# Value products of two heads made together in an attention stage on one core

## The reference

```python
p = softmax(q @ k.T * scale)          # branches B (windowed, with sink), C, D
p = p[:, :, 0] - lam * p[:, :, 1]     # branch A: two score maps per head
o = p @ v                             # 64 value columns per head
```

## Time and profile before

| | |
|---|---|
| median of three runs | 5237.1 us (5235.92 to 5241.41) |
| profiled execution | 5237.16 us, span of its trace 5235.3 us |
| TensorE busy in the span | 5096.8 us, 97% |
| VectorE, ScalarE, GpSimd busy | 62%, 32%, 24% |
| mean granted TensorE clock | 0.986 |
| attention stage, layer one | 290.87 to 546.93: A to 373.15, B to 432.12, C to 488.88, D to 546.93 |
| attention stage, layer two | 2892.18 to 3150.33: A to 2975.85, B to 3035.51, C to 3092.28, D to the end |

### The profile page before, as it was taken

How to read it: one execution, slowest core, us unless ns; L and a number is a source line. 1 busy time by engine, 2 the same in 40 slices (tenths; PEclk the granted TensorE clock), 3 DMA queues, 4 the chain that set the end, 5 groups by cost and what they waited for, 6 DMA issues and landing times.

```text
span 5235.3 us, 68750 instructions
## 1 busy us (share of the span) xinstructions
PE 5096.8 (97%) x25730; PEld 4123.0 (79%) x25730; DVE 3237.9 (62%) x7229; ACT 1682.5 (32%) x2618; POOL 1268.3 (24%) x826
## 2 busy tenths in 40 slices
PE   7999999999999999999999999999999999999999
PEld 4666887788888888888876668868888888888887
DVE  3865211149899876666648652111698998666666
ACT  3344321333333332222233442213333333322222
POOL 1300221224434421111113002202344434111111
PEclk9989999999999999999999899999999999999999
DMA  7100121456787788888820001211577787888886
GB/s 281 34 26 1 48 73 60 189 206 220 264 282 253 246 310 290 290 290 290 288 76 29 26 1 55 70 60 61 205 253 242 268 280 238 319 289 289 289 290 222
DMA packets 349898, 982.01 MB, mean 188 GB/s; under 512 B 31648, under 2 KB 101408, under 8 KB 346272
## 3 DMA queue, kind: packets, MB, share of 16 engines
q1 hardware_dynamic: 216000, 553.19, 31.7%
q0 software_dynamic: 74880, 276.86, 15.3%
q10 hardware_dynamic: 58720, 148.04, 7.2%
HBM read 829.43 MB, written 148.54 MB: 187 GB/s over the span
## 4 chain that ended last, share of the span: by engine, by line
PE 85%; DVE 8%; DMA 2%; ACT 2%; issue 1%; DVEq 1%; ACTq 0%; POOL 0%; POOLq 0%; SPq 0%
PE PS L925 27%; PE PS L882 23%; PE PS L502 14%; PE PS L491 5%; PE PS L906 4%; PE PS L645 3%; PE PS L673 3%; DVE AR L1319 2%; PE PS L657 1%; PE PS L492 1%; PE PS L615 1%; DVE AR L1340 1%; DVE SM L1358 1%; DMA gates_by_expert<-AR 1%; PE PS L828 0%
## 5 line engine op out<-in xcount | busy, mean ns | idle before, releaser
L925 PE MATMUL PS<-HB,VR 128*128 128x512 f32 x6144 | 1394.8, 389 | 3.4 <-DVE HB L1619 3.4
L925 PEld LDWEIGHTS PS<-HB,VR 128*128 128x128 f32 x6144 | 1154.1, 188 | 244.9 <-issue 5.0
L882 PE MATMUL PS<-HR,UR 128*128 128x512 f32 x4128 | 1008.0, 398 | 0.0
L1662 POOL TENSOR_TENSOR UR<-WR,UR 128x1024 fp32r<-128x1024 f32 x212 | 529.5, 2499 | 1822.5 <-ACT UR L1125 945.7
L502 PE MATMUL PS<-HR,UR 128*128 128x320 f32 (+1 forms) x5952 | 914.2, 312 | 14.0 <-DVE HR L1294 9.7
L502 PEld LDWEIGHTS PS<-HR,UR 128*128 128x128 f32 x5952 | 877.3, 188 | 44.4 <-issue 27.4
L882 PEld LDWEIGHTS PS<-HR,UR 128*128 128x128 f32 x4128 | 764.3, 189 | 165.7
L1606 DVE TENSOR_TENSOR VR<-HT,VR 128x1024 fp32r<-128x1024 f32 x256 | 313.7, 1226 | 455.9 <-ACT VR L1244 368.1
L1244 ACT CAST VR<-HT 128x1024 fp32r<-128x1024 f32 x256 | 268.8, 1050 | 960.1 <-PE PS L925 955.9
L882 PE MATMUL PS<-HR 128*128 128x512 f32 x2016 | 486.6, 394 | 0.0
L882 PEld LDWEIGHTS PS<-HR 128*128 128x128 f32 x2016 | 372.1, 188 | 73.5
(11 more groups left out here) (201 smaller groups left out, 6076.4 us busy)
## 6 DMA issues: line engine op xcount, KB each, us to landing
WR<-in_uT SPq DMA_DIRECT2D x256, 512.0 KB
HT<-in_vtab SPq DMA_DIRECT2D x256, 512.0 KB, 4.6
activations<-AR ACTq DMA_DIRECT2D x256, 256.0 KB
gates_by_expert<-AR ACTq DMA_DIRECT2D x128, 512.0 KB, 3.6
HW<-activations SPq DMA_DIRECT2D x256, 256.0 KB
WR<-gates_by_expert SPq DMA_DIRECT2D x64, 1024.0 KB
AR<-in_ada SPq DMA_DIRECT2D x40, 1024.0 KB, 7.6
WR<-in_wgate SPq DMA_DIRECT2D x64, 640.0 KB, 3.9
```

Of the source, the lines that this page charges most:

```text
L882: last = pe.matmul(bank(n % 2), u_part(n, w)[:, c, :], HR[:, h, c, 0:LAT], start=c == 0 and i == 0, stop=c == DC - 1 and i == 2)
L925: last = pe.matmul(bank(d), VR[:, m % 4, w, P * d:P * d + P], HB[:, (m + 1) % 3, h, :], start=m == 0 and i == 0, stop=m == E1 - 1 and i == 2)
L1662: nc.gpsimd.tensor_tensor(dst, src, high.bitcast(F32), ALU.subtract).then_inc(sem_, 1)
```

## The change

The turned probabilities `PT` get four buffers, laid over the space of the split weights `UR`, which is not in use in this stage. `weigh` makes the products of a whole pair: for each key tile head 0's matmul, then head 1's. It is called in every second step, four units behind the scores. The copy `turned` of u waits for the products of the pair that holds u - 4. `turn` waits for normalised probabilities before it waits for the copy, and its unread matmul is gone.

```diff
--- before.py
+++ after.py
@@ -159,6 +159,9 @@
 
         XT = sb("XT", [P, DC, TOK])
         HT = sb("HT", [P, DC, TOK])
+        with nc.sbuf_tensor("turned_probs", [P, 4 * D], F32) as TP:
+            pass
+
         UR = sb("UR", [P, 2, 2, D], F32R)
         WR = sb("WR", [P, RING, SLOT])
         CN = sb("CN", [P, C_ALL])
@@ -235,7 +238,7 @@
         MODR = Arena(AR, AF - 512 * SETS, AF).take(SETS, 512)
         t_ = Arena(AR, shared, AF)
         PB = t_.take(3, 2, 640)
-        PT = t_.take(2, 640)
+        PT = TP[:, 0:4 * 640].rearrange("p (a b) -> p a b", a=4)
         u_ = Arena(AR, shared, AF)
         HSQ, HSTD, HRS = u_.take(2, TOK), u_.take(2, TOK), u_.take(2, TOK)
         g_ = Arena(AR, 0, shared)
@@ -648,30 +651,33 @@
 
             def turn(l, u):
                 br, j, t, hh = units[u]
+                pe.wait_ge(p_ready, l * NU + (u + 1))
                 if u >= 1:
                     pe.wait_ge(pt_ready, l * NU + u)
-                    if br == "A":
-                        pe.matmul(bank(4, 256), ones, CN[:, 0:256], start=True, stop=True)
-                pe.wait_ge(p_ready, l * NU + (u + 1))
                 for i in range(len(key_tiles(br, t))):
                     last = pe.transpose(PF[:, 2048 + P * i:2048 + P * i + P], PB[:, u % 3, 0, P * i:P * i + P], ident)
                 last.then_inc(t_ready, 1)
 
-            def weigh(l, u):
-                br, j, t, hh = units[u]
-                h = 2 * j + hh
-                pe.wait_ge(pt_ready, l * NU + (u + 1))
-                if hh == 0 and u >= 4:
-                    pe.wait_ge(o_done, l * (NU // 2) + (u // 2 - 1))
-                v = {"A": lambda kt: VT[:, kt, 64 * h:64 * h + 64],
-                     "B": lambda kt: VT[:, kt, 256 + 64 * (h // 2):320 + 64 * (h // 2)],
-                     "C": lambda kt: VT[:, kt, 384 + 64 * (h // 2):448 + 64 * (h // 2)],
-                     "D": lambda kt: VD[:, kt, 64 * h:64 * h + 64]}[br]
+            def weigh(l, pair):
+                br, j, t, _ = units[2 * pair]
+                pe.wait_ge(pt_ready, l * NU + 2 * (pair + 1))
+                if pair >= 2:
+                    pe.wait_ge(o_done, l * (NU // 2) + (pair - 1))
+
+                def v(kt, hh):
+                    h = 2 * j + hh
+                    if br == "D":
+                        return VD[:, kt, 64 * h:64 * h + 64]
+                    at = {"A": 64 * h, "B": 256 + 64 * (h // 2), "C": 384 + 64 * (h // 2)}[br]
+                    return VT[:, kt, at:at + 64]
+
                 tiles = key_tiles(br, t)
-                out = PF[64 * hh:64 * hh + 64, 3072 + 512 * (u // 2 % 2):3072 + 512 * (u // 2 % 2) + P]
+                at = 3072 + 512 * (pair % 2)
                 for i, kt in enumerate(tiles):
-                    last = pe.matmul(out, v(kt), PT[:, u % 2, P * i:P * i + P], start=i == 0, stop=i == len(tiles) - 1)
-                last.then_inc(pv_done, 1)
+                    for hh in range(2):
+                        last = pe.matmul(PF[64 * hh:64 * hh + 64, at:at + P], v(kt, hh), PT[:, (2 * pair + hh) % 4, P * i:P * i + P],
+                                         start=i == 0, stop=i == len(tiles) - 1)
+                last.then_inc(pv_done, 2)
 
             pe.wait_ge(c_in, 32)
             pe.wait_ge(cs_ready, 1)
@@ -777,8 +783,8 @@
                         keep_busy(5, 2)
                     if 2 <= s < NU + 2:
                         turn(l, s - 2)
-                    if s >= 3:
-                        weigh(l, s - 3)
+                    if s >= 4 and s % 2 == 0:
+                        weigh(l, (s - 4) // 2)
                 keep_busy(5, 5)
                 phase_end(pe, l, 2)
 
@@ -1031,10 +1037,10 @@
             def turned(l, u):
                 br, j, t, hh = units[u]
                 act.wait_ge(t_ready, l * NU + (u + 1))
-                if u >= 2:
-                    act.wait_ge(pv_done, l * NU + (u - 1))
+                if u >= 4:
+                    act.wait_ge(pv_done, l * NU + 2 * ((u - 4) // 2 + 1))
                 n = P * len(key_tiles(br, t))
-                nc.scalar.copy(PT[:, u % 2, 0:n], PF[:, 2048:2048 + n]).then_inc(pt_ready, 1)
+                nc.scalar.copy(PT[:, u % 4, 0:n], PF[:, 2048:2048 + n]).then_inc(pt_ready, 1)
 
             def modulation_rows(l, which):
 
```

## The result

The changed kernel takes 5295.1 us (median of 4 runs, 5294.6 to 5297.6), the kernel before on the same chip 5239.3 (5235.9 to 5246.8): ratio 1.0108, interval 1.0096 to 1.0121. It is slower, as forecast, by 56 us where 22 were forecast, and 3 us beyond the upper end of the range. The profiled span is 5292.7 us at a mean granted clock of 0.965, before 5235.3 at 0.986.

The account below looks back on a forecast made before the run. C and D were taken as TensorE-bound with the chain close behind, A nearly VectorE-bound, B chain-bound (TensorE at the low clock). −25 us at unchanged clock plus 45 for low clock gave +20 on 5237.1: 5257, rounded to 5259; range 5212 to 5292.

Parts of the forecast that it names:

- Slower, by the clock: Attention stage: thinner TensorE work makes the clock fall more often, mostly in A and B; net +20 us, chance 0.70.
- Twenty records in 1.35 us: Value products: a pair's twenty records, alternating between output halves, take 1.35 us where two units spent 2.48.
- The rival of heads in turn: Value products: the heads do not run at once, 2.45 us stand in the chain, total 5284; chance 0.08.
- The chain holds C and D near 6.1 a pair: C and D: maximum, exp and copy keep pairs at 6.09 and 6.1 us, though TensorE's work falls to about 5.2 and 4.9.
- The gain of 13 us in both at an unchanged clock: C and D, both layers: −5 in C's large pairs, 0 in D's, −8 around the context tile.
- A near 7.5 a pair at the high clock: Branch A: VectorE bounds the pair, 8.06 us falling to 7.5; −9 on 16 pairs, −3 in context units.
- The price of a low us: Loss for each us at the low clock level: 0.25 us in A, 0.31 in B, 0.35 in C.
- How much low time: Low-clock time after, both layers: A 100 us, B 104, C 24, D 6; costing 67, net +45 after today's 22.
- The sum: Whole kernel: −25 us at an unchanged clock, +45 from the low clock, +20 in all: 5257, rounded up to 5259.
- all of A and B with half of C: Upper end for the clock's cost: A and B wholly low and C half low, about +90 us.
- The rival that the clock holds: Attention stage: no further clock falls, −25 us, 5212, or 5190 if today's low stretches vanish too; chance 0.17.
- The prediction's own figure for the waits: TensorE's idle gaps after the change: none expected to pass 1.3 us, against a longest of 0.81 in the rows cited.

Follow-up runs that it names:

- head after head: The change with the pair's products ordered head 0 whole, then head 1 whole, in the same step; 5314.1 against 5239.6 us for the kernel before, ratio 1.0143.
- the kernel with fills: The change plus one unread 512-column product in every odd step of all branches; 5232.2 against 5239.6 us for the kernel before, ratio 0.9991.
- The repeat: The changed kernel run once more, unaltered, for a second trace; 5287.6 us against 5241.1 for the kernel before, one execution each.

## Why the prediction was right, and where it fell short

*Slower, by the clock.* Right in direction, and shown from both sides: the loss comes with the pairing (ratio 1.0086 with the unread products back) and goes with a filled odd step (0.9991). For A the place was right too: in the pairs shown the level fell in the wait behind each odd step, which had lost its value products.

*Twenty records in 1.35 us.* Right: 1.31, and 1.25 to the next scores. The rival of heads in turn falls; head after head costs the 0.7 us a pair that such a fall would bring.

*The chain holds C and D near 6.1 a pair.* Right: 6.01 to 6.05, with TensorE's own 5.18 once the copy went first. The gain of 13 us in both at an unchanged clock was too large, above all around the context tile: starting lengths of 54.4 and 57.3 against 56.8 and 58.1 are 2.4 and 0.8 a layer, 6 in all. The waits of 1.69 us stand just there, at the one-tile units, where the prediction called the chain short. This is an argument from a line through four lengths, not a measurement.

*A near 7.5 a pair at the high clock.* No A of the change had a pair at the high level from end to end. In the kernel with fills VectorE's maxima start at 318.63 and 326.21, 7.58 apart, so the step holds where it can be seen. The pair that took 10.34 was low for 6.8 us of it (clock 0.67), so it lost 0.41 for each low us, where 0.25 stood for a pair low from end to end.

*The price of a low us.* Right in C: 0.33 measured, 0.35 used.

*How much low time.* This is the step that failed. The prediction said "Low time after, for both layers: A 100 (of 150), B 104 (of 130), C 24, D 6", 234 us; the windows give 116, 109, 50 and 11, 286. The largest miss is C. It was priced as if each C fell by itself, for some 12 us; but of its 50 us, 40 are one stretch of layer one that began in B and ran on over the border, with TensorE full at half speed. The repeat shows the same, for 21 us. The C of layer two, which started high, had 9, fewer than forecast. That a low stretch of one branch goes on into the next was no term of the sum. In the kernel with the old order of the copy and unread products in A and B, the level fell inside C, at one-tile units or next to them, and stayed low for some 27 and 31 us, so a C of this code can also lose it by itself. At the prediction's own prices the missing time is 16 × 0.25 + 5 × 0.31 + 26 × 0.35 + 5 × 0.35 = 16 us, 9 of them in C.

*The sum.* The stage grew by 43.7 us where 20 were forecast: 16 more by the low time, 7 by the smaller gain in C and D; the rest is rounding, and A 3 us over and B 4 under their sums. Two slips of adding stand in the prediction: 5 + 16 is 21, not "about 22", and all of A and B with half of C come by its own prices to 38 + 40 + 20 − 22 = +76, not "about +90". The other 12 of the 36 us between 5259 and 5295 lie outside the stage, where the change touches nothing. Between the last branch of layer one and the first of layer two the kernel before took 2892.18 − 546.93 = 2345.3 us, the change 2356.4 and its repeat 2352.6; the other kernels took 2345.3 to 2355.0, both with the value products one head at a time (2345.3 and 2353.5) and paired. Of the 11 us between before and the change, 6.1 are longer waits of TensorE for the split weights that GpSimd writes (9.3 us in place of 3.2), 2.4 a longer wait for `HT` (4.2 and 1.8). Whether that is chance or follows from the clock in which the stage ends wasn't tried, and stays open.

*The rival that the clock holds* falls, and with it, for this kernel, the rule of the Trainium skill, "TensorE: Matmul & The Clock Gate", "Why this matters for your kernels", which ties the low clock to long idle gaps: in A the level fell in every pair of the timeline shown, with idle times of 0.80 and 1.41 us. The runs agree with it as far as this: with the waits of 0.83 and 1.69 us in C gone or shortened to 0.74 by the copy going first, the clock stayed at 1.00. The prediction's own figure for the waits, none above 1.3 us, was passed: 1.41 in A, 2.06 in B ahead of the long low stretch, 2.02 in D.

## What to carry to other kernels

Before shortening TensorE's work in a stage whose clock is already below 1.00, read the clock column and ask what fills the engine there; packed products fill it half as long, and the time that they free is worth nothing while another engine's chain holds the pair. Move the chain first (here one copy ahead of one exp in ScalarE's queue), then pack, then put unread work only where the clock still falls: the first alone gave 0.3%, the second alone cost 1.1%, the two together changed nothing that can be told (0.9998), and all three gained 1.1%. More unread work than fits into idle time costs again: with the copy in its old place, 0.9991 became 1.0039. And look at the branch ahead: a stage can run slowly because the level fell before it began.

## What the runs showed of the hardware that was not expected

- The speed of the pairing was forecast, its dependence on the order was not. Matmuls into two halves of the output partitions, taken turn by turn, ran two at a time: twenty records in 1.31 us at the high level, where ten of one head took 1.31, and in 2.31 to 2.40 where the clock was low for most or all of them. The Trainium skill, "TensorE: Matmul & The Clock Gate", Part 3, gives 2.38 times for three column tiles; here two gave twice the rate. The same twenty, head after head, took 2.02.
- The clock was low for most of a branch whose windows call TensorE 93% busy (62.60 of 67.60 us in C at 0.70). A high busy share is no sign of a high clock: the same records kept it busy for 48.77 us at 0.92. Nor did full work bring the level back: it stayed low for 39.86 us in which TensorE was busy for 39.04.
- In A the level fell and rose again within single pairs of 10.3 us, both ways in the rows shown.
